# Score products with the low part of the keys read 128 partitions in place of 64

## The reference

```
q, k, v, z = split(rmsnorm(x) @ w_in)
scores = einsum(q, band(k)) / 8 - slope * dist     # window of 128, then softmax with a sink
x = x + rmsnorm((softmax(scores) @ band(v) * silu(z)) @ w_out)
```

```
scores = (q_nope @ k_nope.T + q_rope @ k_rope.T) * 192 ** -0.5      # 512 x 512 for each head
o = softmax(scores) @ v
```

## Time and profile before

| | us |
|---|---|
| median of 3 runs (lowest to highest) | 2489.99 (2487.33 to 2490.1) |
| span of the profiled execution | 2484.1 |
| TensorE busy | 2415.9 (97%) |
| weight loads busy | 1909.7 (77%) |
| VectorE busy | 1100.6 (44%) |
| ScalarE busy | 759.7 (31%) |
| GpSimd busy | 258.7 (10%) |
| mean granted clock of TensorE | 0.983 |

### The profile page before, as it was taken

The page is one execution under the profiler, slowest core; times in us unless marked ns, Lnnn a source line. Parts: engine busy times, 40 slices in busy tenths (PEclk is TensorE's granted clock), DMA queues, the critical chain, the costliest instruction groups (busy, mean ns, idle before and its releaser), DMA issues.

```text
span 2484.1 us, 28260 instructions
## 1 busy us (share of the span) xinstructions
PE 2415.9 (97%) x10534; PEld 1909.7 (77%) x10534; DVE 1100.6 (44%) x1410; ACT 759.7 (31%) x1190; POOL 258.7 (10%) x221
## 2 busy tenths in 40 slices
PE   7999999999999999999999999999999999999995
PEld 6777777777888688877777778868888777777884
DVE  7555655556225433334444442262433444445123
ACT  5332333334222331232323242233222332324221
POOL 3100000001113300000000021151000000001113
PEclk9998999999999999999999999999999999999998
DMA  7211111113224322212121142271222212213321
GB/s 281 92 51 68 65 54 68 68 51 127 111 101 183 144 97 102 87 64 87 57 75 55 68 155 100 84 271 68 102 86 82 75 56 83 72 57 119 118 101 68
DMA packets 36357, 238.95 MB, mean 96 GB/s; under 512 B 4160, under 2 KB 4416, under 8 KB 11840
## 3 DMA queue, kind: packets, MB, share of 16 engines
q1 hardware_dynamic: 29520, 204.47, 22.7%
q10 hardware_dynamic: 6336, 25.17, 2.6%
q0 software_dynamic: 432, 8.39, 0.8%
HBM read 221.24 MB, written 16.78 MB: 96 GB/s over the span
## 4 chain that ended last, share of the span: by engine, by line
PE 91%; DVE 4%; issue 2%; DMA 2%; ACT 1%; POOL 0%; ACTq 0%; SPq 0%; DVEq 0%; POOLq 0%
PE acc L444 71%; PE sc L444 4%; PE ov L711 2%; PE ov L543 2%; PE sc L597 2%; PE sc L520 2%; PE sc L519 2%; PE sc L700 1%; PE sc L692 1%; DMA xr<-residual 1%; PE sc L531 1%; DVE g L1086 1%; PE ov L444 1%; PE sc L691 1%; DMA g<-xT_dram 1%
## 5 line engine op out<-in xcount | busy, mean ns | idle before, releaser
L444 PE MATMUL acc<-h_hi,hi 128*128 128x512 f32 x2560 | 1027.6, 401 | 27.4 <-DVE h_lo L1111 15.1
L444 PE MATMUL acc<-h_lo,hi 128*128 128x512 f32 x2560 | 1005.9, 393 | 0.0
L444 PE MATMUL acc<-h_hi,lo 128*128 128x512 f32 x2560 | 1005.7, 393 | 0.0
L1054 DVE TENSOR_TENSOR lo<-raw,hi 128x2048 fp32r<-128x2048 f32 x175 | 388.9, 2222 | 566.0 <-ACT hi L748 563.7
L444 PEld LDWEIGHTS acc<-h_hi,hi 128*128 128x128 f32 x2560 | 486.6, 190 | 141.3 <-issue 23.1
L444 PEld LDWEIGHTS acc<-h_lo,hi 128*128 128x128 f32 x2560 | 487.2, 190 | 103.1 <-issue 5.3
L444 PEld LDWEIGHTS acc<-h_hi,lo 128*128 128x128 f32 x2560 | 486.3, 190 | 104.0
L748 ACT ACTIVATE hi<-raw 128x2048 fp32r<-128x2048 f32 (+2 forms) x178 | 330.7, 1858 | 162.6 <-PE acc L444 157.0
L755 ACT ACTIVATE sq<-acc 128x512 f32<-128x512 f32 x60 | 35.9, 599 | 470.9 <-PE acc L444 470.9
L331 POOL TENSOR_TENSOR sqacc<-sqacc,sq 128x512 f32<-128x512 f32 x74 | 102.3, 1382 | 450.0 <-ACT sq L755 448.2
L408 POOL TENSOR_TENSOR lo<-raw,hi 128x2048 fp32r<-128x2048 f32 x3 | 23.7, 7885 | 1040.0 <-ACT hi L748 1040.0
(11 more groups left out here) (197 smaller groups left out, 2198.8 us busy)
## 6 DMA issues: line engine op xcount, KB each, us to landing
raw<-w_dram SPq DMA_DIRECT2D x162, 1024.0 KB, 4.6
raw_m<-wm_dram SPq DMA_DIRECT2D x16, 1024.0 KB, 6.3
xr<-residual ACTq DMA_DIRECT2D x16, 512.0 KB, 6.0
residual<-g ACTq DMA_DIRECT2D x16, 512.0 KB, 6.0
raw<-w_dram SPq DMA_DIRECT2D x8, 896.0 KB, 4.3
g<-xT_dram SPq DMA_DIRECT2D x4, 1024.0 KB, 12.0
residual<-g POOLq DMA_DIRECT2D x1, 4096.0 KB, 13.8
area<-memT_dram POOLq DMA_DIRECT2D x2, 2048.0 KB, 11.6
```

Of the source, the lines that this page charges most:

```text
L444: ins = pe.matmul(to, a, b, start=first and n == 0, stop=last and n == 2)
L1054: dve.tensor_tensor(lo[c.slot][:, 0:width], raw[c.slot][:, 0:width], hi[c.slot][:, 0:width].bitcast(F32), ALU.subtract).then_inc(lo_done, 1)
```

## The change

In both places the slice that picks one half of the partitions is dropped, from the stationary and from the moving operand. The second matmul then reads the high and the low part of the queries against the low part of the keys, and so adds q_lo x k_lo as well. Nothing else is changed.

```diff
@@ -517,7 +517,7 @@
                         to = bank(2 * par + b // 2, 256, b % 2 * 256)
                         q, k = tile(par * TB + b, P), slice(b * P, b * P + 256)
                         pe.matmul(to, q1[:, q], k_hi[:, k], start=True, stop=False)
-                        ins = pe.matmul(to, q1[HALVES[par], q], k_lo[HALVES[par], k], start=False, stop=True)
+                        ins = pe.matmul(to, q1[:, q], k_lo[:, k], start=False, stop=True)
                 ins.then_inc(scores1, 1)
 
@@ -686,10 +686,10 @@
                     pe.wait_ge(v_done, l * (MLA // 2) + (i + 1))
                     pe.wait_ge(qk_done, no)
                     for b in range(TB):
-                        q, r64 = tile(b, P), HALVES[j]
+                        q = tile(b, P)
                         passes(bank(b), qn_hi[:, q], qn_lo[:, q], kn_hi[:, :], kn_lo[:, :], True, False)
                         pe.matmul(bank(b), qr[:, q], kr_hi[:, :], start=False, stop=False)
-                        ins = pe.matmul(bank(b), qr[r64, q], kr_lo[r64, :], start=False, stop=True)
+                        ins = pe.matmul(bank(b), qr[:, q], kr_lo[:, :], start=False, stop=True)
                     ins.then_inc(scores2, 1)
```

## The result

The changed kernel takes 2388.78 us (median of 4 runs, 2387.24 to 2392.34), the one before beside it 2488.66 (4 runs, 2481.91 to 2490.1). The ratio is 0.9609, 95% interval 0.9593 to 0.9624. Forecast were 2392 us in a range of 2384 to 2414. The profiled run took 2389.51 us with a span of 2387.6; the mean granted clock is 0.991, against 0.983.

A forecast was written before the change was run, and what follows sets the result against it. TensorE's stream was taken to bound the kernel (91% of the chain). Switches in the first layer 51.0, in the heads 25.6 and the clock 21.4 sum to 98.0 us: 2489.99 to 2392 us, range 2384 to 2414.

The forecast's parts named there:

- Step 1: First-layer scores, 16 calls: spacing falls to 0.12 us without partition-count switches, 51.0 us saved.
- Step 2: Latent heads' scores, 64 blocks: each falls from 1.53 to 1.13 us without switches, 25.6 us saved.
- Step 3: First layer, behind the scores: ten half-rate clock stretches go, 21.4 us saved.
- Rival A: First layer: half-rate stretches stay, since value products have a part in them; 2413 us with ten as now, 12 in 100.
- What is late next: Softmax between scores and transposes: no new wait, cost 0; margins 1.4 us in first layer, 0.97 in heads.
- Rival B: Softmax: a VectorE or ScalarE step is longer than read, TensorE waits at the transposes; 2415 us, 4 in 100.
- The sum of the span: Whole kernel: 98.0 us off the profiled span, from 2484.1 to 2386.1 us.
- Rivals C and D: Scores: spacing not from switch, 2490 us, 2 in 100; or products slower without row change, 2534 us, 1 in 100.

The follow-up runs named there:

- grouped kernel: Kernel before with its 64-partition products kept but reordered into groups in first layer and heads, for fewer partition-count changes: 2402.31 us, ratio 0.9654.
- two all on 64 partitions: Kernel before with all first-layer score products on 64 partitions, q_lo x k_hi left out, halves in turn or lower first: 2414.3 and 2414.98 us.
- thin kernel: Changed kernel with each product of scores_first cut into eight of 32 columns, all on 128 partitions: 2781.21 us.
- heads alone: Kernel before with only the latent heads' product with kr_lo put on 128 partitions: 2461.52 us, ratio 0.9889.

## Why the prediction was right

*What was changed and what bounds.* Right: TensorE's stream shortened, and the span followed it. Forecast were 98.0 us of the span, measured 96.5.

*Step 1, the changes in the first layer.* The spacing of 0.12 us came as in the earlier trace rows. The call is 2.01 us and not 1.92, since the 0.10 us behind its first load, which isn't run ahead, weren't counted; the step behind it fell from 0.34 to 0.23. That makes 16 x 3.10 = 49.6 of the forecast 51.0 us. What the prediction called the cause (the change of the partition count, about 0.2 us each way, against 64 partitions as such) was argued from two rows then. The grouped kernel shows it: with the same products and fewer changes most of the time goes. The two all on 64 partitions show that such products need 0.12 us each when no change stands between them.

*Step 2, the heads.* 26.2 us against 25.6: 1.60 us a call as forecast, and 0.07 more in every second one.

*Step 3, the clock.* The ten stretches behind the scores are gone. From the first call to the end of the last, 492.0 us became 420.7: 71.3, of which 49.6 are step 1 and 21.7 the clock, against 21.4. That the thin stretch was the cause stood on their coincidence; the thin kernel shows a fall with no change of the count in it, and the heads alone show that the stretches don't come and go by themselves. Rival A is out: the products of the values still run ahead of the scores, and the clock stays up.

One reading in this step was wrong. Not every stretch begins at the end of a call or in its last microsecond: the four long ones begin 0.9, 1.9, 2.7 and 3.5 us ahead of it. The windows of the fourth in the kernel before, from the call's start to the fall and behind it:

```profile
217.48:220.30 2.82, 2.82 (x10) 1.66 (x9) 2.77 (x3) 0.38 (x1) 0.47 (x2) 1.00 0.00 0
220.30:227.20 6.90, 6.90 (x16) 4.65 (x16) 3.86 (x4) 0.00 (x0) 1.84 (x3) 0.51 0.43 152
```

The clock fell after 2.8 us of such products and not after 5, and in the thin kernel after 2.3 us at the soonest. Calls of 2.0 us were thus nearer to it than the prediction believed. They are both shorter and denser than before, and no run tells which of the two kept the clock up.

*What is late next.* Nothing. The rows that answer to the earlier trace rows, VectorE and then TensorE, first layer and one of the tight heads:

```profile
265.79 2.19 DVE L1178 TENSOR_SCALAR prob<-prob,st 128x256 f32<-128x256 f32 x8
...
269.38 1.69 PE L531 MATMUL sc<-cst,prob 128*128 128x128 f32 x14
```

```profile
1182.74 2.29 DVE L1438 TENSOR_REDUCE st<-sc 128x4 f32<-128x2048 f32 x1 [0.28 <-PE sc L692]
1188.31 1.67 DVE L1444 TENSOR_SCALAR prob<-prob,st 128x512 f32<-128x512 f32 x4
...
1190.71 1.91 PE L700 MATMUL sc<-cst,prob 128*128 128x128 f32 x16
```

In the first layer the probabilities are ready at 267.98, 1.40 us ahead of the transposes, as forecast; only the first pair has less, 0.43 us. In the heads VectorE's wait fell from 1.77 to 0.28 us, and 0.73 us are left of the 0.97, where the prediction saw no loss: part of what a call gains lies behind its last product, so the transposes come nearer to the last score product by 0.31 to 0.36 us and VectorE's start by 0.11 only. Rival B is out, but half of the first layer's margin is used: VectorE's work is bound by its own split there, so 1.4 us more taken from that stream, and the softmax is late.

*The sum of the span.* 71.3 + 26.2 = 97.5, and about 1 us is lost elsewhere. The first scores start 0.36 us later. From the last call of the first layer to the first head it takes 2.0 us longer, with a half-rate stretch that is in both kernels and is longer after. Behind that 1.4 us come back. The windows of that stretch, before and after:

```profile
600.00:615.00 15.00, 10.93 (x41) 8.55 (x40) 10.18 (x10) 6.47 (x12) 5.16 (x2) 0.89 0.37 137
```

```profile
530.00:545.00 15.00, 10.93 (x37) 8.45 (x36) 10.09 (x10) 5.44 (x10) 4.57 (x2) 0.77 0.47 170
```

Rivals C and D fell with the spacing of 0.12. The 5.9 us that the prediction set between the span and the runs were no constant: every run on record with a span of its own lies 1.9 to 2.0 us above it, so the profiled execution of the kernel before was about 4 us faster than the median. That, and not a step, is most of the distance from 2392 to 2388.8.

## What to carry to other kernels

Count the changes of the partition count in TensorE's stream before counting products: a product on half of the partitions, put between full ones, cost about 0.4 us more here than one that reads twice as much. If the operands stand in both halves anyway, let it read all of them; if it must stay on 64, group such products, and let lower and upper half take turns, here with different banks of PSUM. And look at the granted clock behind thin stretches: TensorE's busy share was 100% through all of them, and a fifth of this gain came from the clock.

## What the runs showed of the hardware

Changing between 128 and 64 partitions costs about 0.2 us each way, in two parts: 0.09 us before the first product of the new kind and 0.11 behind it (0.32 and 0.33 to 0.34 us in place of 0.23 between starts of 512 columns). The same two parts stand at the start of a call of scores_first in the changed kernel, where no partition count changes: 0.32 us into it (251.38 to 251.70) and 0.22 in place of 0.12 behind its first product. What the two places share is a weight load that isn't run ahead.

Products on the lower and on the upper 64 partitions start together when they stand in turn, here writing different banks: sixteen in 1.15 us. The upper half's began four products ahead of their turn when the lower half's stood first.

GpSimd's copy of k_hi (L382) all but stands still while VectorE splits weights (L1054). Before, it ran beside L1161 and took 0.62 us. In the changed kernel it begins 1.15 us before a split ends (253.01 to 255.30) and takes 1.63; with the first layer all on 64 partitions in turn it begins 2.09 us before (248.48 to 250.77) and takes 2.57. In both 0.48 us are left behind the split. Only GpSimd's next copies wait for it. Before, changed, and all on 64 in turn:

```profile
257.34 0.62 POOL L382 CAST k_hi<-k_hi_all 128x512 fp32r x1 [4.88 <-PE sc L520]
```

```profile
254.15 1.63 POOL L382 CAST k_hi<-k_hi_all 128x512 fp32r x1 [1.98 <-PE sc L520]
```

```profile
248.68 2.57 POOL L382 CAST k_hi<-k_hi_all 128x512 fp32r x1 [1.05 <-PE sc L520]
```
